# Order of the Strassen sums in two seven-product stages, and two added waits on GpSimd

## The reference

```python
h = rmsnorm(x, g_mix_pre[l])
z = h @ w_in[l]                       # the projection ("z stage")
...
x = x + rmsnorm(mix, g_mix_post[l])
f = conv_glu_ffn(rmsnorm(x, g_ffn_pre[l]), w_up[l], conv_w[l], conv_b[l], w_down[l])
x = x + rmsnorm(f, g_ffn_post[l])

def conv_glu_ffn(h, w_up, conv_w, conv_b, w_down):
    u = h @ w_up                      # 1024 -> 2 x 2816
    u = depthwise causal convolution of width 3 over tokens, plus conv_b
    a, b = jnp.split(u, 2, axis=-1)
    return (jax.nn.gelu(a, approximate=True) * b) @ w_down
```

## Time and profile before

| what | value |
|---|---|
| median of three runs | 3151.39 us (3147.83 to 3151.8) |
| the profiled execution, its own time | 3153.93 us |
| its span, first to last instruction | 3152.2 us |
| granted TensorE clock, mean | 0.993 of full speed |
| PE, DVE, ACT, POOL busy | 97%, 65%, 47%, 38% of the span |

### The profile page before, as it was taken

The page is one execution under the profiler, slowest core; times in us unless marked ns, Lnnn a source line. Parts: engine busy times, 40 slices in busy tenths (PEclk is TensorE's granted clock), DMA queues, the critical chain, the costliest instruction groups (busy, mean ns, idle before and its releaser), DMA issues. The chain is left out here.

```text
span 3152.2 us, 44863 instructions
## 1 busy us (share of the span) xinstructions
PE 3048.0 (97%) x16138; PEld 2482.5 (79%) x16138; DVE 2063.1 (65%) x3931; ACT 1468.7 (47%) x2657; POOL 1202.5 (38%) x840
## 2 busy tenths in 40 slices
PE   8999999999888999999999999999999999999998
PEld 8888888887767766766678778888888788888887
DVE  5565565556768977877744687777555477777343
ACT  5332443236767866666633444444434344444332
POOL 2444244310000024442110198888110688885010
PEclk9999999999999999999999999999999999999999
DMA  4464545376666623431144522221565222223553
GB/s 142 163 187 144 176 156 172 124 209 224 240 222 240 184 69 83 134 89 43 61 114 126 170 87 81 90 84 67 187 218 186 97 83 92 81 80 113 185 196 107
DMA packets 274811, 433.90 MB, mean 138 GB/s; under 512 B 125760, under 2 KB 178240, under 8 KB 261568
## 3 DMA queue, kind: packets, MB, share of 16 engines
q1 hardware_dynamic: 265600, 395.70, 38.1%
q0 software_dynamic: 8992, 35.33, 3.4%
HBM read 312.51 MB, written 126.84 MB: 139 GB/s over the span
## 5 line engine op out<-in xcount | busy, mean ns | idle before, releaser
L1111 PE MATMUL z_banks<-ops,z_area 128*128 128x512 f32 x1720 | 434.1, 391 | 3.2 <-DVE z_area L858 3.2
L3194 PE MATMUL f_banks<-f_wt 128*128 128x512 f32 x1776 | 406.1, 389 | 0.0
L3194 PEld LDWEIGHTS f_banks<-f_wt 128*128 128x128 f32 x1776 | 333.3, 188 | 69.2
L1111 PEld LDWEIGHTS z_banks<-ops,z_area 128*128 128x128 f32 x1720 | 322.9, 188 | 70.3 <-DVE z_area L858 3.6
L2564 POOL TENSOR_TENSOR f_wt<-f_wt_f,f_wt 128x1024 fp32r<-128x1024 f32 x132 | 316.1, 2418 | 64.6 <-ACT f_wt L2695 59.1
L2043 ACT ACTIVATE w_small<-w_small,a_stats 128x128 f32<-128x128 f32 (+3 forms) x510 | 256.2, 516 | 90.5 <-DVE a_stats L2128 63.2
L3165 PE MATMUL f_banks<-low,f_wt 128*128 128x512 f32 x704 | 274.0, 389 | 0.0
L2986 DVE SCALAR_TENSOR_TENSOR near<-w_small,vk,near 128x1024 f32<-128x1024 f32 x88 | 231.2, 2628 | 1.7
L2128 DVE CUSTOM_DVE_ANT_0 w_small<-a_s_ps,near 128x128 f32<-128x128 f32 (+2 forms) x456 | 164.5, 392 | 89.2 <-PE a_s_ps L1929 79.1
L1973 PE MATMUL a_ot_ps<-a_turned_w,vs 128*64 128x256 f32 (+3 forms) x1452 | 221.3, 428 | 0.0
L3165 PE MATMUL f_banks<-f_oo,f_wt 128*128 128x512 f32 x704 | 217.0, 390 | 2.5 <-ACT kc_f L2729 1.2
(11 more groups left out here) (306 smaller groups left out, 7079.4 us busy)
## 6 DMA issues: line engine op xcount, KB each, us to landing
low<-z_parts SPq DMA_DIRECT2D x46, 1024.0 KB, 6.2
f_wt_f<-in_w_ffn SPq DMA_DIRECT2D x74, 512.0 KB, 4.1
z_area_f<-in_w_z SPq DMA_DIRECT2D x54, 512.0 KB, 5.1
f_raw_f<-in_w_ffn SPq DMA_DIRECT2D x22, 1024.0 KB, 4.8
f_wt_f<-in_w_ffn SPq DMA_DIRECT2D x22, 1024.0 KB, 5.3
g_up<-near SPq DMA_DIRECT2D x44, 512.0 KB, 2.6
f_wt_f<-g_up SPq DMA_DIRECT2D x88, 256.0 KB, 4.3
z_parts<-z_st_hi SPq DMA_DIRECT2D x68, 256.0 KB, 2.3
```

What stands on the lines that cost most here:

```text
L1111: last = pe.matmul(banks[:, bank, :], w[:, c * P:(c + 1) * P], rows[:, c * 512:(c + 1) * 512], start=(first and c == 0 and q == 0), stop=( ...
L3194: last = pe.matmul(banks[:, 2 * t + n, :], g[:, tok], w[:, n, :], start=(d == 0 and x == 0), stop=(d == NF - 1 and x == 2))
```

## The change

In the z stage S4 is formed before S3, and the wait of DVE's first lower part goes from four sums to three. In the FFN the order S1, S3, S2, [lower part of A11], S4 becomes S1, S2, [lower part of A11], S4, S3; ACT's upper part of S1 and S2 waits for two sums instead of three. For n = 2, 3, 24 and 25 POOL waits for `add_p6(n - 1)` before S1. For step 0, ACT makes the upper part of S1 and S2 before `upper_b(0, 3)` instead of behind it.

```diff
@@ project, sums_a
                 pool.tensor_tensor(s2, s1, raw[:, 0], ALU.subtract).then_inc(s_done, 1)
-                pool.tensor_tensor(s3, raw[:, 0], raw[:, 2], ALU.subtract).then_inc(s_done, 1)
                 pool.wait_ge(s_done, done + 2)
                 pool.tensor_tensor(s4, raw[:, 1], s2, ALU.subtract).then_inc(s_done, 1)
+                pool.tensor_tensor(s3, raw[:, 0], raw[:, 2], ALU.subtract).then_inc(s_done, 1)
@@ project, lower_a
                 if first == PZS1:
-                    dve.wait_ge(s_done, 4 * pairs_before(g) + 4)
+                    dve.wait_ge(s_done, 4 * pairs_before(g) + 3)
@@ mix_ffn, sums_a
                     pool.wait_ge(p_done, 7 * (n - 1))
+                if n % NF in (2, 3):
+                    pool.wait_ge(ev_done, 5 * (n - 1) + 1)
                 pool.tensor_tensor(lo[:, S1], raw[:, 2], raw[:, 3], ALU.add).then_inc(s_done, 1)
-                pool.tensor_tensor(lo[:, S3], raw[:, 0], raw[:, 2], ALU.subtract).then_inc(s_done, 1)
                 pool.wait_ge(s_done, 4 * n + 1)
                 pool.tensor_tensor(lo[:, S2], lo[:, S1], raw[:, 0], ALU.subtract).then_inc(s_done, 1)
@@ mix_ffn, sum_b
-                pool.wait_ge(s_done, 4 * n + 3)
+                pool.wait_ge(s_done, 4 * n + 2)
                 pool.tensor_tensor(lo[:, S4], raw[:, 1], lo[:, S2], ALU.subtract).then_inc(s_done, 1)
+                pool.tensor_tensor(lo[:, S3], raw[:, 0], raw[:, 2], ALU.subtract).then_inc(s_done, 1)
@@ mix_ffn, upper_s12
-                act.wait_ge(s_done, 4 * n + 3)
+                act.wait_ge(s_done, 4 * n + 2)
@@ mix_ffn, ACT's order for step 0
                     upper_a22(0)
+                    upper_s12(0)
                     upper_b(0, 3)
-                    upper_s12(0)
                     upper_s34(0)
```

## The result

The changed kernel takes 3155.93 us (median of 22 runs, 3152.91 to 3158.56), the kernel before 3150.15 us beside it (22 runs, 3147.83 to 3152.06): a ratio of 1.0018, interval 1.0011 to 1.0024, so 5.8 us slower (3.5 to 7.6). The profiled execution took 3154.04 us.

A forecast was written before the change was run, and what follows sets the result against it. PE was taken to bound the kernel, busy 3048.0 of 3152.2 us. Terms of -0.2 (z), +0.9 (first half) and +2.3 (second half) made +3.0 on the median 3151.39: 3154.4 us, range 3143.5 to 3160.0.

The forecast's parts named there:

- S3 behind the lower part of A11: FFN opening steps: POOL's moved S3 makes PE start later, +0.9 us in the first half, +2.5 in the second; steady step 0.
- hold, first half: Steps 2 and 3: POOL's wait for `add_p6` nearly ends the stall at (2,5), with (2,2) 0.95 us late: -4.8 us.
- hold, second half: Steps 23 and 24: the same wait gives back 3.37 + 2.5 us with remainders of 0.7 + 0.25: -5.0 us.
- late next: From steps 3 and 25: POOL's lateness makes `add_p7` 2.4 us late at (3,5), repeated at steps 25, 26: +4.8 us each half.
- The openings: At (1,1), (22,1) and (23,1), PE waits about 1 us longer for POOL's lower parts.
- z: Item 14 of the z stage: S3 still runs before DVE's lower part, so only -0.2 us.
- ACT's order: Step 0: POOL's lower part still waits for `first_lower` on DVE, so 0 us, bounds -1.4 and +0.1.
- full shared time: Steady FFN step: POOL's 13.6 us and DVE's contested 5.5 make 19.1, as long as a step; lateness has almost no spare time.
- the end of the sum: Whole kernel: +3.0 us put on the median 3151.39 gives 3154.4; from the profiled execution's own time, 3156.9.
- Rival (a): Steps 3 and 25: POOL's lateness is harmless, no stalls at (3,5) and (25,5): -6.6 us, 3144.8; chance 0.28.
- Rival (b): Opening steps 1 and 23: the clock falls to 0.50 near 1833 or 2503: +8.0 us, 3159.4; chance 0.13.
- Rival (c): Held steps: `add_p6` is done when POOL arrives, so only the moved sums count: +3.2 us, 3154.6; chance 0.04.

The follow-up runs named there:

- h1: The changed kernel with two of POOL's lower-part operations in step 3 (and 25) cut to 8 of 512 columns a block: 3150.71 us, ratio to before 1.0001.
- g2: The kernel before with only ACT's new order for step 0 (`upper_s12(0)` ahead of `upper_b(0, 3)`): 3150.88 us, ratio 0.9998.
- e5: The kernel before with only the z stage's new order and shorter wait: 3149.08 us, ratio 0.9996.
- e3: The changed kernel with POOL's hold also in a further step of each half (n % 22 in 2, 3, 4): 3157.87 us, ratio to before 1.0026.
- e2: The kernel before with only POOL's two-line wait for `add_p6` added, sums in the old order: 3154.94 us, ratio 1.0015.
- e1: The changed kernel without POOL's two-line wait for `add_p6`, the moved sums kept: 3151.41 us, ratio to before 1.0005.
- f1: The kernel before with DVE's `gate(n - 1)` moved from ahead of `add_p7(n)` to between `add_p7` and `add_p5`: 3142.94 us, ratio 0.9972.
- e4: The kernel before with DVE's `gate(n - 1)` moved from ahead of `add_p7(n)` to behind `add_p5(n)` in every step: 3166.29 us, ratio 1.0053.

## Why the prediction was right, and where it was wrong

The forecast was 3154.4 us, inside 0.2% of the kernel before, and the measured 3155.93 lies there too. That the two are only 1.5 us apart is partly luck: the change was put at +3.0 us and came at +5.8, and the median of three runs that it was added to lay 1.24 us above that of 22. (0.2% is also not the least that can be told from no change: 22 runs a side told 0.18%.) The mechanism held place by place. To see its terms one by one, each product's time from its start to the next product's start in the kernel after is set against the kernel before, in both profiles of the latter:

| term | forecast | against the first profile | against the second |
|---|---|---|---|
| S3 behind the lower part of A11, at steps 0, 1, 22, 23 | +0.9 + 2.5 | +3.13 | +3.17 |
| hold, first half: (2,5) with its low clock, (2,2) | -4.8 | -4.64 | -3.25 |
| hold, second half: (23,5), (24,2), (24,5) | -5.0 | -5.11 | -4.09 |
| late next: (3,2), (3,5), (4,5) | +4.8 | +4.86 | +4.86 |
| late next: (25,2), (25,5), (26,5) | +4.8 | +4.95 | +4.95 |
| sum in the openings | +3.2 | +3.19 | +5.64 |

(Differences under 0.08 us are left out; with them the sums are 3.25 and 5.62. The first row holds 0.2 us that step 0 gained at (0,5).)

**The openings** came as forecast: (1,1), (22,1) and (23,1) wait for POOL, 0.9 to 1.2 us longer than before. **The hold and what is late next** too: (2,5) and (23,5) without idle time, POOL waiting for `add_p6` 4.37 us, then (3,5) late by 2.14 (forecast 2.4) with a further 1.63 at (4,5) (forecast 1.3), and at (25,5) 2.15 with the low clock (1.7, from 3.40 us at 0.50). The forecast left open which of the two follows; each came once. (2,2) and (3,2) waited 0.57 and 0.28 us where 0.95 and 0.7 had been put, but cost 0.94 and 0.57 from start to start: a wait of PE costs some 0.3 us beyond its idle time. **z** and **ACT's order** gave what was put, nothing that can be measured.

Two things in the working don't hold as written. Its "+5.1 from step 3 on" is not the sum of its terms (0.7 + 2.4 + 1.7 = 4.8). And the full shared time counts five operations of DVE a step, but the two `edge` copies of 128x2 share it too: in h1 they took 1.65 and 2.29 us (at 1874.73 and 1885.89), in the steady step of the kernel before 0.55 (at 1895.19).

**The step that failed** is the end of the sum, with the hold's -4.8 and -5.0 under it. They were taken from one execution, in which each of the two stalls was followed by a low clock of 2.5 us and more, and the sum was then put on the median of the runs, to which that execution stood 2.54 us above. Part of what made it slower was the very low clock that the hold was credited with removing, so it was counted twice. In the second profile the same stalls cost 2.4 us less, the two terms are -7.3 instead of -9.8, and the sum is +5.6, with z's -0.2 +5.4; the runs gave +5.8. From the execution's own time the prediction had 3156.9, from the median 3154.4; the measured 3155.93 lies between. g2 and e5 add two more profiles of these steps: against the four, the openings of the changed kernel are 3.25, 5.62, 4.42 and 6.94 us longer, 5.1 in the mean, and the runs' interval of 3.5 to 7.6 leaves out the first alone. The changed kernel has one profile, and four don't say how often each low clock comes.

**Rival (a), lateness that is harmless,** fell: e3 moves the stall on by a step with its size, and h1 takes it away by giving POOL time, as the estimate of a full shared time (13.6 + 5.5 for a step of 19.04 us) had it. The Trainium skill (SBUF — State Buffer, Summary: rules for kernel authors) tells that where a DVE operation has two inputs in SBUF and GpSimd's reads SBUF, the second one to issue blocks until the first finishes, and to schedule whichever is off the critical path. h1's operation of 16 elements and 1.20 us agrees with the first half. For the second, e2 is the measurement: holding POOL cost 4.7 us (1.0015, 1.0006 to 1.0023); the reading, which e3 and h1 bear out, is that in a full step neither engine is off the path for long. **Rival (b), the clock at the openings,** did not come: no low clock shows between 1828 and 1833 or 2497 and 2504. **Rival (c), a hold that never waits,** fell with the 4.37 us. Its price of +3.2 can be read all the same, as e1 is that kernel: 1.6 us, since PE's lateness at (1,1) and (23,1) comes in part off its idle time at (2,5) and (23,5).

What the parts cost adds up against the second profile of before: the openings grow by 1.5 us with the moved sums (e1), 4.0 with the hold (e2) and 5.6 with both. With single profiles that spread by 3.7 us this is no proof; the medians give 1.6, 4.7 and 5.8. The stalls inside do not add: the moved sums alone already take (2,5) from 2.72 to 1.47 and (23,5) from 3.38 to 2.16 and bring 1.63 each at (3,5) and (24,5).

Left open: which executions get a long low clock, a short one or none behind the same idle time.

## What to carry to other kernels

Where two engines block one another and their contested time fills a step, as here, holding one back moved a stall on and added the hold's own waits (e2, e3). What helped was the order on the engine on which PE waits, so that the operation PE needs goes ahead of one that nobody waits for at once (f1: 8 us for a few lines moved); one place further (e4) it cost 16 us. A gain that consists of a slower clock must be taken against an execution's own time, or from several profiles of the same kernel, and never put on the median of the runs.

## What the runs showed of the hardware

Equal idle times of PE were followed by unequal low clocks. After 2.72 us at (2,5), the next 5.20 us had 12 matmuls at 0.50 in one profile of before and 16 at 0.70 in another; after 3.38 us at (23,5) the clock fell in the first two profiles of before and stayed at 1.00 in e5; after 2.14 us at (3,5) of the kernel after it stayed up, after 2.15 us at (25,5) of the same execution it fell. At item 14 of z, after some 3 us, the stretch of 4.8 us had 0.64 in the earlier trace rows and 1.00 in the kernel after, whose wait was 0.3 us shorter; but h1, with the same z stage as the kernel after, has its low clock there too (0.64). Each such fall is worth some 1.5 to 2.6 us, as much as most terms of this change.

DVE and POOL block one another even where an operation is tiny: a POOL operation of 16 elements a partition took 1.20 us behind DVE's taps, and DVE's copy of 2 elements took 2.36 us behind POOL (e4) and 0.55 us in the steady step of the kernel before.
